# RWKV token mixing: the kept part computed by ScalarE from PSUM, and the raw products of a head pair issued two groups to a step

## What is computed

```python
def _rwkv_prepare(z, mu, ...):
    zp = jnp.pad(zf, ((0, 0), (1, 1), (0, 0)))
    zf = zf + (0.5 * (zp[:, :-2] + zp[:, 2:]) - zf) * f(mu)     # token mixing: (1 - mu) z + mu/2 (left + right)
    r, k, v, w_lo_f, w_lo_b, a_lo_f, a_lo_b, g_lo = _split(zf, ...)
    ...
def _wkv_scan(r, w, k, v, kk, a, s0, reverse):
    def step(S, inp):
        sa = jnp.einsum('bhvk,bhk->bhv', S, kk_t)
        S = S * w_t - sa * (kk_t * a_t) + v_t * k_t
        return S, jnp.einsum('bhvk,bhk->bhv', S, r_t)
def _rwkv_out(y, r, v, ks, g, r_k, gn_w, gn_b, dtype):
    # group norm of y per head, plus a bonus term times v, times the gate g
```

## Time and profile before

| what | value |
|---|---|
| median of three runs | 2586.5 us (2586.43 to 2590.49) |
| profiled execution, time | 2591.72 us |
| profiled execution, span | 2589.9 us |
| PE busy | 2490.4 us, 96% of the span |
| DVE busy | 805.2 us, 31% |
| ACT busy | 574.8 us, 22% |
| POOL busy | 233.7 us, 9% |
| mean granted TensorE clock | 0.984 of full |
| first and second layer's pairs | about 507 to 990 us, and about 1860 to 2245 us |

### The profile page before, as it was taken

The page is one execution under the profiler, slowest core; times in us unless marked ns, Lnnn a source line. Parts: engine busy times, 40 slices in busy tenths (PEclk is TensorE's granted clock), DMA queues, the critical chain, the costliest instruction groups (busy, mean ns, idle before and its releaser), DMA issues. The chain is left out here.

```text
span 2589.9 us, 46521 instructions
## 1 busy us (share of the span) xinstructions
PE 2490.4 (96%) x20808; PEld 1476.5 (57%) x20808; DVE 805.2 (31%) x1651; ACT 574.8 (22%) x1233; POOL 233.7 (9%) x243
## 2 busy tenths in 40 slices
PE   6999999999999999999999999999999999999998
PEld 4444654455555554444444445556466667687887
DVE  2542333253444432121010002441555554321101
ACT  3353323122223211020000002441332323111100
POOL 0000000122222300000000000010022323000000
PEclk9999999999999999999999999999999899899999
DMA  7102111233232334222222224112122111145443
GB/s 285 50 17 73 42 57 49 90 105 110 67 139 68 132 111 151 73 98 81 74 75 79 73 81 151 49 66 90 41 83 67 51 59 60 61 138 177 154 155 106
DMA packets 64391, 238.81 MB, mean 92 GB/s; under 512 B 7009, under 2 KB 8049, under 8 KB 63425
## 3 DMA queue, kind: packets, MB, share of 16 engines
q1 hardware_dynamic: 61824, 220.23, 25.1%
q0 software_dynamic: 2368, 15.61, 1.6%
HBM read 234.76 MB, written 1.05 MB: 91 GB/s over the span
## 5 line engine op out<-in xcount | busy, mean ns | idle before, releaser
L420 PE MATMUL psum<-normed,panel_ring 128*128 128x512 f32 (+1 forms) x3136 | 1166.4, 517 | 5.1 <-ACT normed L648 4.1
L420 PEld LDWEIGHTS psum<-normed,panel_ring 128*128 128x128 f32 x3136 | 575.6, 191 | 425.6 <-issue 374.0
L420 PE MATMUL psum<-arena,panel_ring 128*128 128x512 f32 (+1 forms) x1792 | 609.8, 494 | 1.8 <-ACT arena L1067 1.8
L420 PE MATMUL psum<-arena 64*64 64x64 f32 (+5 forms) x12696 | 522.0, 251 | 41.6 <-ACT arena L739 10.3
L420 PEld LDWEIGHTS psum<-arena 64*64 64x64 f32 (+2 forms) x12696 | 343.3, 141 | 334.1 <-issue 214.6
L420 PEld LDWEIGHTS psum<-arena,panel_ring 128*128 128x128 f32 x1792 | 335.2, 191 | 225.7 <-issue 200.3
L714 DVE TENSOR_REDUCE softmax_stats<-psum 128x1 f32<-128x512 f32 (+1 forms) x144 | 83.8, 600 | 178.8 <-PE psum L420 177.7
L739 ACT ACTIVATE arena<-psum,softmax_stats 128x512 f32<-128x512 f32 (+1 forms) x144 | 87.7, 613 | 220.0 <-PE psum L697 111.0
L1819 DVE TENSOR_TENSOR arena<-arena 128x512 f32<-128x512 f32 (+1 forms) x64 | 35.8, 559 | 305.8 <-ACT arena L1806 305.8
L1695 DVE SCALAR_TENSOR_TENSOR arena<-psum,modulation,arena 128x256 f32<-128x256 f32 x24 | 10.9, 480 | 313.9 <-PE psum L420 313.9
L1571 POOL TENSOR_SCALAR arena<-arena 128x64 f32<-128x64 f32 x96 | 72.2, 766 | 323.2 <-DVE arena L1617 178.1
(11 more groups left out here) (159 smaller groups left out, 1379.2 us busy)
## 6 DMA issues: line engine op xcount, KB each, us to landing
panel_ring<-panels SPq DMA_DIRECT2D x398, 512.0 KB, 3.3
arena<-panels SPq DMA_DIRECT2D x16, 512.0 KB, 14.8
arena<-small_b POOLq DMA_DIRECT2D x2, 2176.0 KB, 9.9
arena<-bias_d POOLq DMA_DIRECT2D x2, 2048.0 KB, 9.2
arena<-x_t SPq DMA_DIRECT2D x2, 1024.0 KB, 7.4
arena<-x_t POOLq DMA_DIRECT2D x1, 2048.0 KB, 14.4
arena<-const_r POOLq DMA_DIRECT2D x2, 800.0 KB, 6.6
arena<-small_c POOLq DMA_DIRECT2D x2, 768.0 KB, 4.7
```

The costliest lines, as they stand in the source:

```text
L420: return nc.tensor.matmul(out, lhsT, rhs, start=start, stop=stop, skip_group_check=check)
```

## The change

Two things. In `stage_c`, ACT now computes the kept part itself from PSUM, with mu's column as its scale, ahead of its copy into `pad`; DVE's tensor_scalar is gone, and only its add is left. In the core, the number of RAW steps goes from 8 to 4: steps are merged two and two, on each engine by moving a `yield`. The `close` of the pair before is placed two steps to a tick, in the first four ticks. All 77 or 78 filler steps of a core are now spread over 38 ticks, 2.04 to a tick.

```diff
-PREP, RAW, LEVEL_STEPS, SCAN, CLOSE = 17, 8, 2 * (LEVELS - 1), 3 * NCH, 8
+PREP, RAW, LEVEL_STEPS, SCAN, CLOSE = 17, 4, 2 * (LEVELS - 1), 3 * NCH, 8
...
                 if c >= 2:
                     e.wait_ge(neighbours.h, c - 1)
-                    e.wait_ge(kept.h, c - 1)
+                    e.wait_ge(mixed.h, c - 1)
+                sg = slice(1, 2) if lat_only(j) else slice(0, 2)
+                nc.scalar.activation(two(kept_part[:, c % 2, :])[:, sg, :], two(ps)[:, :sg.stop - sg.start, :], ACT.Copy,
+                                     scale=drv[:, l, 24 + j:25 + j]).then_inc(kept.h, 1)
...
-                turns.wait_freed(e, n)
-                if c >= 2:
-                    e.wait_ge(mixed.h, c - 1)
                 o = two(kept_part[:, c % 2, :])[:, sg, :]
-                nc.vector.tensor_scalar(o, pad[:, c % 2, sg, 1:CTX + 1], drv[:, l, 24 + j:25 + j], None, ALU.mult).then_inc(kept.h, 1)
                 e.wait_ge(kept.h, c + 1)
                 e.wait_ge(neighbours.h, c + 1)
...
             to_tokens((0, 1), lambda d: v).then_inc(s_v.h, 1)
-            yield
             e.wait_ge(s_op.h, s_op.at(3))
...
                 p.then_inc(raw_full.h, 1)
-                yield
+                if n == 0:
+                    yield
             e.wait_ge(raw_dve.h, raw_dve.at(1))
...
                 p.then_inc(raw_full.h, 1)
-                yield
+            yield
             e.wait_ge(raw_act.h, raw_act.at(2))
             to_tokens((0, 1), lambda d: be[:, d, :]).then_inc(raw_full.h, 1)
-            yield
             e.wait_ge(raw_act.h, raw_act.at(3))
...
             p.then_inc(s_vc.h, 1)
             yield
-            yield
-            yield
             for n, (dst, bank) in enumerate(((nt, 2), (m13[:, :, 0:4], 0), (m13[:, :, 4:8], 2), (bt, 0), (kt, 2))):
...
-                yield
+                if n % 2 == 0:
+                    yield
...
-            yield from idle(5)
+            yield from idle(3)
...
         def core_dve(e):
-            yield
             e.wait_ge(s_eye.h, s_eye.at(1))
...
-            yield from idle(RAW - 3)
+            yield from idle(RAW - 2)
...
-                if p and tick < CLOSE:
-                    place(pairs[p - 1][2], 1)
+                if p and tick < CLOSE // 2:
+                    place(pairs[p - 1][2], 2)
```

More of the change, by code:

```diff
@@ L1561, in core_pool @@
                 p.then_inc(masked.h, 1)
-                yield
-            yield from idle(RAW - 7 + LEVEL_STEPS)
+            yield
+            yield from idle(RAW - 4 + LEVEL_STEPS)
             link(e, nc.gpsimd.tensor_scalar(bonus, kssum, col("r_k", ft), None, ALU.mult))
```

## The result

The changed kernel takes 2607.0 us (median of 4 runs, 2603.7 to 2611.4) against 2586.5 (4 runs, 2582.3 to 2590.5): ratio 1.0082, interval 1.0061 to 1.0104, 20.5 us slower. Later, on another chip and beside other kernels, it took 2611.1 against 2585.4: 1.0109, 1.0082 to 1.0135.

The account below looks back on a forecast made before the run. PE was taken as the bound. Terms of -11.2 (round trips), +24.0 (closing waits), +15.3 (clock), +7 (levels) and +1 (start, attention) gave +36 on 2586.5: 2622 us, range 2610 to 2634, wide range 2598 to 2645.

Parts of the forecast that it names:

- Round trips: PE switching between core and filler: 32 fewer round trips at 0.35 us each, -11.2 us (0 to -11.2).
- The two waits of a closing: PE waits at mean (2.3, 2.05 us) and sums of squares (1.95, 1.7), three closings a layer: +24.0 us (18 to 28).
- The clock: PE's granted clock dips behind nine of twelve new closing waits, 1.7 us each: +15.3 us (0 to 36).
- Levels: PE's waits for level transposes and copies, 11 panels for 8, each held longer: +7 us (-15 to +15).
- the later add: POOL's add on a panel starts one ACT operation later, holding DVE's queue 0.35 us longer.
- more panels among the levels: Panels of pairs 1 and 2 ending among level steps rise from 8 to 11, at 1.5 us of wait each before.
- the longer filler: 2.04 filler steps a tick for 1.83 give 0.18 us more cover in layer 0; 1.6 us taken off.
- 3.4 us after ACT begins: Sign of being right: transposes of levels with a panel start this long after ACT begins, DVE's idle time growing.
- the start: First prep of layer 0 waits 0.35 us longer; with six panels in layer 1's last attention, +1 us (0 to 4).
- the clock stays out of it: Rival, chance 0.15: no clock dips follow the new waits, sum +21, 2607 us.
- The levels were not cured: Refers to the rival, chance 0.10, that level waits and their dips vanish: 35.8 us won, sum -7, 2580 us.

Follow-up runs that it names:

- e1: The kernel before with only the kept part moved to ACT, ahead of the padded copy: 2590.0 us, 1.0025 to before.
- e3: The changed kernel with the close placed one step to a tick in eight ticks: 2574.8 us, 0.9953 to before.
- e11: The changed kernel with the close placed 1, 3, 2, 2 steps in the first four ticks, covering only the mean: 2577.3 us, 0.9963 to before.
- e12: The changed kernel with the close placed 2, 1, 1, 2, 2 in the first five ticks, covering only the squares: 2593.1 us, 1.0029 to before.
- a2: The changed kernel run again unaltered on another chip, as base for e11, e12 and e13: 2611.1 us, 1.0109 to before.
- e2: The changed kernel with the kept part on DVE again, so the merged steps alone: 2596.9 us, 1.0057 to before.
- e4: The changed kernel with ACT's padded copy ahead of the kept part, POOL's add waiting only for that copy: 2597.7 us, 1.0055 to before.
- e13: The changed kernel with close one step to a tick, padded copy first, and DVE's part of a panel two steps later: 2548.2 us, 0.9856 to before.
- e10: The changed kernel with close one step to a tick and the kept part left on DVE: 2563.3 us, 0.9923 to before.
- e6: The kernel before, eight RAW steps unmerged, their filler doubled in every second tick (20 fewer round trips): 2584.9 us, 1.0003 to before.

## Why the prediction was right, and where its sizes were off

**Round trips.** -11.2 forecast; net busy time of PE is 13.1 us less in the changed kernel. Over all profiles, the eleven with merged steps have 2436.2 us in the mean (2434.3 to 2438.9), and the two with eight RAW steps and filler in each (before and e1) 2447.2: -11.0, or 0.34 us for each of the 32. Right.

**The two waits of a closing.** +24.0 forecast, +22.2 measured: 2.2 and 1.9 us for 2.3 and 2.05, 1.7 and 1.6 for 1.95 and 1.7. I had added the semaphore on top of operations that in a row overlap by 0.1 us. The place, the engines and the count were right, and e3, e11 and e12 show each wait going when its cause is taken away.

**The clock.** +15.3 forecast, 8.7 between the two profiles, 9 and 19 between the medians of all runs: the term is real, and no run shows that its size was wrong. Its working was. Nine dips were set behind the twelve new waits; seven came (12.0 us), in a2 six, and in e2 and e4, which have the same twelve waits, six and five: half of 48. And I held the dips elsewhere unchanged. They were not: the dip of 10.2 us at 2205, behind a 1.66 us stall in the middle of a group that no semaphore explains, and four short ones of layer 0 are gone, and in layer 1 dips of 6.8 us at 2050 and 2156 and two smaller ones stand where one of 6.8 at 2027 stood. Away from the closings the pairs lost 5.1 us less, and the stages outside the pairs 1.8 us more. A dip is tied to one wait in one execution and not to a kernel. Runs of the changed kernel went from 2603.7 to 2617.6.

The clock moves with the waits by more than their own length in some pairs of kernels (12.2 us in e12 for 9.8 us of waits), but single executions of the kernel before differ by more than that, so this is no rule.

**Levels.** +7 forecast, +5.3 measured (12.7 to 18.0). Half of the reasoning holds: e1, in which no panel moves, shows +5.3, and e4 takes 5.9 back, so the later add costs the 3.9 us that I had for it (11 x 0.35) and more. The other share, more panels among the levels less the longer filler (4.5 - 1.6 us), is 1.8 us by e2, where the steps are merged and the add is not later. Here is the worst case, in the changed kernel, ACT, POOL, DVE and PE:

```profile
2045.68 0.69 ACT L1140 ACTIVATE arena<-psum,derived_vectors 128x512 f32<-128x512 f32 x1 [4.26 <-PE psum L420]
2046.26 0.59 ACT L1145 ACTIVATE arena<-psum 128x512 f32<-128x512 f32 x1
...
2046.93 1.04 POOL L1120 TENSOR_TENSOR arena<-arena 128x512 f32<-128x512 f32 x1 [16.38 <-ACT arena L1145]
...
2048.07 0.75 DVE L1164 SCALAR_TENSOR_TENSOR arena<-arena,derived_vectors 128x512 f32<-128x512 f32 x1 [3.52 <-POOL arena L1120]
2048.74 0.70 DVE L1589 STREAM_TRANSPOSE arena<-arena 128x512 f32<-128x512 f32 x1
...
2050.94 1.93 PE L420 MATMUL psum<-arena 64*64 64x32 f32 x64 [3.17 <-DVE arena L1591]
```

DVE is idle 3.52 us, and held for 3.06 us from ACT's start to the transposes. I had 3.38, and "3.4 us after ACT begins" among the signs of being right: that sign failed. I took the add at 1.02 us, as long as it was there before, and it took 0.75.

The Trainium skill, page "SBUF — State Buffer", section "SBUF: two separate sides", says that a VectorE operation in a mode that takes both of its ports and a GpSimd operation exclude each other: whichever starts first keeps the shared pair for its whole length. The trace of before agrees, as far as the lengths go (the two start within 0.2 us of each other): L1162 took 1.37 us in most places beside POOL's add of 1.04, and in two places 0.49 us, where POOL's add took 1.27 and 1.33 instead. With the operation gone DVE did get that time back (35 us less busy in e1), and PE nothing.

**Not forecast.** PE's waits for ACT's `ada_rows` ahead of the small transposes fell from 9.6 to 5.9 us in layer 0. That longer filler blocks separate them from their products is the likely cause, not shown by a run of its own.

**The sum.** Outside the clock the forecast was -11.2 + 24.0 + 7 + 1 = +20.8 us; the profiles have 24.1 - 13.1 = +11.0. No single term fails: the round trips gave 1.9 more, the closings cost 1.8 less, the levels 1.7 less, `ada_rows` 3.7 less, and what is left (0.7) is the start and small waits. All misses fell on the same side.

**The rivals.** 2607.0 us is to the microsecond the time of "the clock stays out of it". That is a coincidence of sizes, not its mechanism: seven dips stand behind the new waits, and the clock gave away more in the changed kernel in every comparison. By the time alone the forecast and this rival could not have been told apart. The levels were not cured in this kernel, but e13 shows that more than half of their waits can be: against e3, whose close stands alike, level waits fell from 19.1 to 6.6 us and the time by 26.6, where the rival had 35.8 for all of them with their dips. The kept part on ACT is a loss ahead of the padded copy (e1; e3 against e10); that it is a gain behind it is not shown.

## What to carry to other kernels

When steps that meet on several engines are merged, write down for every wait what stands between the product and the work that it waits for, on the waiting engine and on the one that is waited for: merging saves the fixed cost of going to filler and back, and takes away the filler that hid the answer. Put ahead in each queue what another engine waits for, the operation that starts the longest chain first: the padded copy before the scaled one, as e4 shows. The sum for the mean before the masks would be the same repair for the first closing wait; it was not run. And an engine's queue should not reach an operation before its operand is there: moving the add by two steps was worth 9 us (7 of them outside the clock), while making DVE's part 35 us shorter was worth nothing.

## What the runs showed of the hardware

- Going from 64-row products to 128-row filler and back costs TensorE about 0.3 us beside the work in both (0.34 us by the mean of eleven profiles against two, 32 round trips; 0.32 in e6, 20 round trips).
- Single waits of 1.5 to 2.2 us at the closings were followed by the lower granted clock in half of the cases (24 of 48 in the changed kernel, a2, e2 and e4), 1.7 us of work lost each time. Dips of 5.1 to 10.2 us stood behind level waits of 1.9 to 3.2 us and behind stalls of 1.6 to 2.0 us. Which waits are hit differs between executions of one kernel (seven and six of the same twelve).
- What the clock gives away is most of the spread between runs: 18.0 to 54.6 us for the kernel before, whose spans less that stay within 2543.8 and 2557.3 us.
- VectorE's `tensor_scalar` of 512 float32 columns took 1.37 us beside a GpSimd add and 0.49 us in the two places where the add was the one to be held (1.27 and 1.33 us in place of 1.04).
- Stalls of PE, mostly in the middle of a group of like products and up to 2.0 us long (e6), appear in every trace with "issue" as their cause. They go with the place in PE's own stream: counted in PE's rows from the start, one of 0.73 us stands behind row 884 and one behind row 11926 in all fourteen profiles, others behind row 18254 in nine of them (1.66 us in before, the stall at 2205; 0.33 to 0.88 elsewhere) and behind row 9041 in the three with eight RAW steps (1.50, 1.58 and 2.00 us). No run here tells what they are.
